# A hybrid RWKV-7 / neighbourhood-attention step: the first modulation moves from VectorE to TensorE

## The reference, cut to what matters

```python
def modulation(cond, w_ada, b_ada):            # w_ada: 1024 x 6144
    m = jax.nn.silu(cond) @ w_ada + b_ada
    return jnp.split(m[..., None, :], 6, axis=-1)

sh1, sc1, g1, sh2, sc2, g2 = modulation(cond, lp['w_ada'], lp['b_ada'])
h = rmsnorm(x, lp['norm1_g']) * (1 + sc1) + sh1
z = h @ lp['w_in']                             # then RWKV-7, attention, w_out, ConvFFN
```

## Time and profile before

| what | value |
|---|---|
| time, median of 3 runs | 2557.2 us (2552.21 to 2563.93) |
| the profiled execution | 2560.71 us, its span 2558.7 us |
| TensorE busy | 2397.7 us, 94% of the span |
| VectorE, ScalarE, GpSimd busy | 52%, 28%, 26% |
| granted TensorE clock, mean | 0.981 |

### The profile page before, as it was taken

How to read it: one execution, slowest core, us unless ns; L and a number is a source line. 1 busy time by engine, 2 the same in 40 slices (tenths; PEclk the granted TensorE clock), 3 DMA queues, 4 the chain that set the end, 5 groups by cost and what they waited for, 6 DMA issues and landing times.

```text
span 2558.7 us, 50522 instructions
## 1 busy us (share of the span) xinstructions
PE 2397.7 (94%) x21498; PEld 1966.3 (77%) x21498; DVE 1331.7 (52%) x2126; ACT 720.0 (28%) x1179; POOL 654.0 (26%) x283
## 2 busy tenths in 40 slices
PE   1799999999999998889999998999999999999997
PEld 1677778788888887788855687788888888888886
DVE  7755656536467667896543323634333433443344
ACT  3272736444355554333300001201100110011002
POOL 0220210111111111222100243344343434444341
PEclk9899999999999999999989998999999999999998
DMA  6312131112257777676513310011111111011112
GB/s 250 103 53 73 45 108 54 35 74 77 97 171 195 207 202 207 179 209 177 175 66 113 118 42 25 25 42 35 41 41 34 42 34 42 33 42 34 41 34 91
DMA packets 225583, 234.50 MB, mean 92 GB/s; under 512 B 143922, under 2 KB 178866, under 8 KB 224946
## 3 DMA queue, kind: packets, MB, share of 16 engines
q1 hardware_dynamic: 200114, 229.54, 28.4%
q10 hardware_dynamic: 25344, 3.15, 0.8%
HBM read 173.79 MB, written 57.02 MB: 90 GB/s over the span
## 4 chain that ended last, share of the span: by engine, by line
PE 84%; DVE 8%; issue 3%; ACT 2%; DMA 1%; ACTq 1%; POOL 1%; SPq 0%; DVEq 0%; POOLq 0%
PE PS L860 21%; PE PS L862 20%; PE PS L861 20%; PE PS L1301 5%; PE PS L969 3%; PE PS L941 2%; PE PS L955 1%; DVE buffer L1997 1%; DVE buffer L1996 1%; PE PS L943 1%; PE PS L1021 1%; DVE buffer L1796 1%; ACTq L1671 1%; PE PS L1111 1%; PE PS L872 1%
## 5 line engine op out<-in xcount | busy, mean ns | idle before, releaser
L860 PE MATMUL PS<-buffer,buffer 128*128 128x512 f32 (+1 forms) x2784 | 1007.0, 362 | 21.0 <-POOL buffer L2269 8.3
L862 PE MATMUL PS<-buffer,buffer 128*128 128x512 f32 (+1 forms) x2784 | 998.1, 359 | 0.0
L861 PE MATMUL PS<-buffer,buffer 128*128 128x512 f32 (+1 forms) x2784 | 998.0, 358 | 0.0
L860 PEld LDWEIGHTS PS<-buffer,buffer 128*128 128x128 f32 x2784 | 527.0, 189 | 114.7 <-issue 19.3
L862 PEld LDWEIGHTS PS<-buffer,buffer 128*128 128x128 f32 x2784 | 526.9, 189 | 83.6
L861 PEld LDWEIGHTS PS<-buffer,buffer 128*128 128x128 f32 x2784 | 527.1, 189 | 82.6 <-issue 1.0
L2278 POOL TENSOR_TENSOR buffer<-buffer,buffer 128x1024 fp32r<-128x1024 f32 x76 | 184.3, 2424 | 836.2 <-PE PS L862 528.6
L2225 DVE SCALAR_TENSOR_TENSOR buffer<-PS,buffer,buffer 128x512 f32<-128x512 f32 (+1 forms) x264 | 158.5, 656 | 156.0 <-PE PS L862 156.0
L2279 POOL TENSOR_TENSOR buffer<-buffer,buffer 128x1024 fp32r<-128x1024 f32 x76 | 193.4, 2545 | 6.0
L2201 DVE TENSOR_SCALAR buffer<-buffer,buffer 128x1281 f32<-128x1281 f32 x22 | 34.4, 1566 | 292.7 <-ACT buffer L1752 292.7
L1752 ACT ACTIVATE buffer<-PS 128x512 f32<-128x512 f32 (+1 forms) x66 | 30.0, 529 | 514.7 <-PE PS L862 514.7
(11 more groups left out here) (217 smaller groups left out, 2802.3 us busy)
## 6 DMA issues: line engine op xcount, KB each, us to landing
buffer<-in_w_up SPq DMA_DIRECT2D x44, 512.0 KB, 3.3
buffer<-in_w_in SPq DMA_DIRECT2D x42, 512.0 KB, 5.0
ops_kept<-buffer SPq DMA_DIRECT2D x40, 512.0 KB, 5.1
buffer<-ops_kept SPq DMA_DIRECT2D x80, 256.0 KB, 3.5
buffer<-in_w_ada SPq DMA_DIRECT2D x32, 512.0 KB, 7.2
buffer<-rkv_kept SPq DMA_DIRECT2D x120, 128.0 KB, 3.4
buffer<-in_w_down SPq DMA_DIRECT2D x22, 512.0 KB, 3.3
buffer<-in_x SPq DMA_DIRECT2D x20, 512.0 KB, 9.8
```

What stands on the lines that cost most here:

```text
L860: mm(out, w_hi, x_hi, start=start, stop=False)
L861: mm(out, w_hi, x_lo, start=False, stop=False)
L862: return mm(out, w_lo, x_hi, start=False, stop=stop)
```

## The change: what it does

**The first modulation.** `w_ada`'s first 2048 columns are handed over in another order, `w_ada_first`: eight chunks of 1 MB, each with all 1024 input features (on partitions, in 8 blocks) for 256 output columns; chunk c holds columns of the shift for even c and of the scale for odd c, so that chunks 2m and 2m+1 serve the feature blocks 2m and 2m+1 of `h`. The conditioning vectors come as 16 more columns of the parameters. TensorE multiplies: for each chunk 8 float32 matmuls with the SiLU vector padded to 32 columns as weights and 256 columns of `w_ada` as the moving operand, the blocks k and k+4 into PSUM partitions 32*(k mod 4) and on (`modulation_parts`). VectorE copies the four partial rows out of PSUM (`parts_copied`), and TensorE adds and turns them with a 0/1 matrix of 2 columns (`modulation_sums`, two float32 matmuls). VectorE adds the bias (`modulation`) and makes the scales of a pair (`first_scale`).

**Order.** `x` is loaded before the chunks. TensorE makes the partial products of chunks 0 and 1 and their sums, and then for each pair m the partial products of the next pair's chunks, the transposes of block 2m, the sums, and the transposes of block 2m+1. ScalarE evicts the first and the middle segment, VectorE the last.

**Moved.** The broadcast load of the conditioning vectors and their SiLU (still needed for the other 32 blocks) now come behind the first stage: the load is issued after the last chunk's, the sigmoid comes after ScalarE's last rounding, the product after VectorE's last subtraction, and SyncE waits for it before it enters the loop. The first Q, K and V tiles are loaded ahead of that wait, and GpSimd splits them as soon as the last chunk's sums are made (`ada_made` 16); the query buffer is cleared after that.

**Places.** `FREE` is rounded up to a multiple of 16 words (64 bytes).

```diff
-        FREE = keep.at
+        FREE = -(-keep.at // 16) * 16
...
             for b in range(TB):
                 sp.dma_start(x10[:, b, :], dram["x"][b]).then_inc(tiles_moved[b // 2], 16)
+            def load_first(c):
+                if c >= 4:
+                    sp.wait_ge(ada_made, parts_made(c - 4))
+                sp.dma_start(ada_first[c % 4].rearrange("p k n -> p (k n)"), dram["w_ada_first"][c]).then_inc(ada_in[c % 4], 16)
+            for c in range(8):
+                load_first(c)
+            sp.wait_ge(sumsq_done, TB)
+            sp.dma_start(cond_raw.rearrange("p c k -> p (c k)"), dram["cond"].to_broadcast([P, 2 * D])).then_inc(cond_in, 16)
...
+            load_qkv(0)
+            sp.wait_ge(h_done, 3 * KB)
+            sp.wait_ge(cond_ready, 2)
...
+            def modulation_parts(c):
+                pe.wait_ge(ada_in[c % 4], 16 * (c // 4 + 1))
+                if c >= 2:
+                    pe.wait_ge(ada_used, sums_made(c - 2))
+                for k in range(KB):
+                    at = 32 * (k % 4)
+                    ins = mm(PS[at:at + 32, 6 + c % 2, 0:2 * P], cond_pad[:, k, :], ada_first[c % 4][:, k, :], start=k < 4, stop=k >= 4)
+                ins.then_inc(ada_made, 1)
+            def modulation_sums(c):
+                pe.wait_ge(ada_used, parts_made(c))
+                for b in range(2):
+                    ins = mm(PS[:, 6 + c % 2, 2 * P + 2 * b:2 * P + 2 * b + 2], ada_parts[c % 2][:, b * P:(b + 1) * P], sum_parts,
+                             start=True, stop=True)
+                ins.then_inc(ada_made, 1)
...
+            for m in range(KB // 2):
+                more = (2 * m + 2, 2 * m + 3) if m + 1 < KB // 2 else ()
+                for c in more:
+                    modulation_parts(c)
+                transposed(2 * m)
+                for c in more:
+                    modulation_sums(c)
+                transposed(2 * m + 1)
...
-            for n in range(ADA_FIRST):
-                if n == 11:
-                    dve.wait_ge(sumsq_done, TB + 1)
-                    V.link(dve.reciprocal(tokstat[:, 1, :], tokstat[:, 1, :]))
-                    for b in range(TB):
-                        ts(diag[:, b, :], ident, tokstat[:, 1, b:b + 1], None, ALU.mult).then_inc(diag_ready, 1)
-                V.link(ada_product(mod[:, n, :], 0, half, ada_spare))
-                ada_product(mod[:, n, :], 1, half, ada_spare).then_inc(ada_used, 1)
...
+            for m in range(KB // 2):
+                more = (2 * m + 2, 2 * m + 3) if m + 1 < KB // 2 else ()
+                for c in more:
+                    parts_copied(c)
+                last_segment(2 * m)
+                if m >= 1:
+                    rest_of_h(2 * m - 1)
+                for c in more:
+                    modulation(c)
+                if more:
+                    first_scale(m + 1)
+                last_segment(2 * m + 1)
+                rest_of_h(2 * m)
             rest_of_h(KB - 1)
+            dve.wait_ge(act_steps, 2)
+            tt(silu, silu, cond_raw, ALU.mult).then_inc(cond_ready, 1)
...
+            pool.wait_ge(consts_in, 32)
+            pool.wait_ge(ada_made, 16)
+            split_qkv(0)
+            pool.wait_ge(h_done, 3 * KB)
+            G.link(pool.memset(qbd[:, :, :], 0.0))
+            with G.loop(1, NP, 3) as i:
+                split_qkv(i)
```

More of the change, by code:

```diff
@@ L255, in build @@
         assert s2.at <= WORDS - 4 * D
-        ada_first = view(LO_AT, 4, 2 * D)
-        cond_raw = view(LO_AT + 8 * D, 2, D)
+        e1 = Space(UPPER)
+        ada_first += [e1(KB, 2 * P), e1(KB, 2 * P), view(WORDS - 4 * D, KB, 2 * P)]
+        e1 = Space(s2.at)
+        cond_sig = e1(KB, 2)
+        cond_pad = e1(KB, P // 4)
+        ada_parts = [e1(2 * P) for _ in range(2)]
+        assert e1.at <= WORDS - 4 * D
         ada_ring = [view(WORDS - 4 * D, D), view(WORDS - 3 * D, D), view(SCR_AT, D), view(SCR_AT + D, D)]
@@ L600, in attention @@
                 sp.dma_start(dram["new_v"][bass.ds(i, 1)].rearrange("a b s c -> s (a b) c"), vtok[:, 0:2, :]).then_inc(newkv_out, 16)
-            with sp.Fori(0, NP) as i:
+            with sp.Fori(0, NP - 1) as i:
                 attention(i)
+                sp.wait_ge(proj_done, (i + 1) * PROJ + 1)
+                load_qkv(i + 1)
+            attention(NP - 1)
             def load_tile(s, src, split=None):
@@ L862, in split_mm, with transposed @@
                 return mm(out, w_lo, x_hi, start=False, stop=stop)
-            pe.wait_ge(diag_ready, TB)
-            for k in range(KB):
+            def modulation_parts(c):
[12 more added lines that the diff above has]
+                ins.then_inc(ada_made, 1)
+            def transposed(k):
                 for g, (t0, n) in enumerate(SEGS):
@@ L1818, in scale_with_gain, with first_scale @@
                     .then_inc(ev, 1)
-            mod_blocks(0, ADA_FIRST)
-            dve.wait_ge(mod_done, 1)
-            scale_with_gain(gsc1, 8, "norm1", gsc_ready)
-            dve.wait_ge(gsc_ready, 1)
+            def first_scale(m):
+                dve.wait_ge(ada_used, sums_made(2 * m + 1))
+                part = gsc1[:, 2 * m:2 * m + 2, :]
+                V.link(ts(part, mod[:, KB + 2 * m:KB + 2 * m + 2, :], 1.0, None, ALU.add))
+                tt(part, part, par("norm1")[:, 2 * m:2 * m + 2].unsqueeze(2).to_broadcast([P, 2, 2]), ALU.mult).then_inc(gsc_ready, 1)
             def rest_of_h(k):
@@ L2260, in _, with split_qkv @@
             G = Steps(pool, pool_steps)
-            pool.wait_ge(h_done, 3 * KB)
-            pool.wait_ge(consts_in, 48)
-            G.link(pool.memset(qbd[:, :, :], 0.0))
-            with G.loop(0, NP, 3) as i:
+            def split_qkv(i):
                 for s in range(3):
@@ L2418 @@
         "w_ada": one["w_ada"].T.reshape(48, P, D),
+        "w_ada_first": one["w_ada"][:, 0:2 * D].reshape(KB, P, 2, 4, 2 * P).transpose(3, 2, 1, 0, 4).reshape(8, P, KB * 2 * P),
         "cond": np.concatenate([a["c_ctx"], a["c"][0]]).reshape(1, 2 * D),
```

142 lines of the change are left out of this document (83 added, 59 removed).

## The result

| what | before | after |
|---|---|---|
| median, us | 2556.1 (2552.2 to 2563.9, 4 runs) | 2516.6 (2510.9 to 2520.1, 4 runs) |
| profiled execution, its span | 2560.71, 2558.7 | 2510.91, 2509.1 |
| ratio | | 0.9839, 95% interval 0.981 to 0.9869 |

The change makes the kernel 39.5 us faster in medians.

What follows compares the result with a forecast made beforehand. TensorE, busy 94%, was taken as the bound, idle mainly before the bias product, where VectorE bounds 20 to 30 us. First stage 23 us, buffer places nothing: 2560.71 less 23 is 2537.7, in medians 2534; range 2500 to 2550.

Steps and rivals of the forecast that it cites:

- Loads, norms, diagonals: Start of the first stage: `x` loaded by 19.0 us, diagonals ready at 25.3 in place of 44.4.
- Partial products: TensorE's `w_ada` chunks in the first stage: 0.95 us each, twice that after TensorE idles; bounds 0.9 and 3.45.
- Column groups don't overlap: Rival on the first stage's chunks: 3.45 us each, so gain only 10 us, time 2547; chance 8%.
- Start of the splits: First stage: GpSimd begins its six splits of Q, K and V tiles at 47.8 us.
- The collision: Splits slow VectorE's five last low parts of `h`; TensorE starts projecting at about 65 us, bounds 58 and 69.
- No collision: Rival: GpSimd and VectorE interleave without loss; gain 31 us, time 2526 to 2527; chance 7%.
- SiLU and the `w_ada` loop: After the low parts: SiLU product done at 69, VectorE's products at about 97, TensorE waiting 1.5 us for them.
- First stage in all: Up to the bias product: it moves from 120.27 to about 97, 23 us gained, bounds 18 to 31.
- The places of the buffers: All split matmuls: moving inputs to a 64-byte multiple gains nothing; bounds 134 us gained to 26 us lost.
- Same place, steady stream: Rival: weights and inputs placed alike speed matmuls outside attention by up to 3.8 ns; 15 us, time 2519; chance 18%.
- The new places hurt: Rival: inputs and weights both on the multiple collide and slow each stream; 26 us lost, time 2560; chance 5%.
- 16 bytes off cost an extra beat per line: Rival on split matmuls: aligning the inputs gains the full 134 us, time 2400; chance 7%.

Runs made afterwards that it cites:

- inputs_16_far: The changed kernel with `FREE` 16 bytes past a multiple of 256, as in the kernel before; 2544.0 us in one run, against 2554.3 for the kernel before.
- before_64: The kernel before with `FREE` alone rounded up to 64 bytes, first stage unchanged; 2530.2 us against 2556.15, ratio 0.9892.
- after_16: The changed kernel with `FREE` 16 bytes past a multiple of 64; 2531.8 us, ratio 0.9912 to the kernel before.
- before_ring_16: The kernel before with `WORDS` raised so the ring's weight tiles stand 16 bytes past a multiple of 64; 2523.7 us against 2557.9, ratio 0.9865.
- after_24: The changed kernel with `FREE` left unrounded, 24 bytes past a multiple of 64; 2545.6 us, ratio 0.9956 to the kernel before.

## Why the prediction came out as it did

- **Loads, norms, diagonals.** Right: 25.1 against 25.3. The DMA engines ran at 425 GB/s here, a little over the 408 of the earlier trace rows.
- **Partial products.** Right: 1.07 and 1.93 against 0.95 and 1.9, from the one row with 64x64 quadrants; but idle time just before a chunk isn't what makes it slow, as the two chunks of 3.48 show. "Column groups don't overlap" is out.
- **Start of the splits.** Right: 47.88 against 47.8.
- **The collision.** Right in kind, short in size. Four of the five low parts came to 2.9 to 3.5, and "No collision" is out. But I counted only the five low parts. The two four-column scale operations have SBUF operands alone, they too waited 2.06 and 2.25, and they stand ahead of the last evictions; the first projection came at 69.5, past the 65 taken and half a microsecond past the bound of 69. The Trainium skill, "SBUF — State Buffer", section "SBUF: two separate sides", states that an operation of VectorE shares the port with GpSimd if it has two SBUF inputs or runs in a mode that uses two ports, and that the later one then waits for the whole instruction. The trace agrees: the PSUM evictions kept their 0.80, and each small operation ended with a split. I had reckoned with the two inputs alone; of the small operations one (L1881) has a single SBUF input beside its constants, and it waited like the other. Whether it ran in such a mode no row shows.
- **SiLU and the `w_ada` loop.** Right in kind: SiLU product done at 71.1 (69 forecast), bias product at 99.1 (97 forecast), the third load late. It was later than I had it: VectorE idles 2.45 for it. TensorE waited 0.2 us for VectorE, not 1.5, because it started its projections 4.5 later than forecast.
- **First stage in all.** 23 us forecast, at least 18. In the two spans 21.0. But kernels with the new first stage had the bias product at 99.1 to 102.8 in nine profiles, those with the old one at 118.0, 118.6 and 120.1; and inputs_16_far, the changed kernel with before's pitches, is 10 us below the kernel before on its chip (2544.0, one run, against 2554.3). The first stage is worth 10 to 21 us, 13.5 as the remainder of the medians (39.5 less the 26.0 of before_64), so my 23 was too much by several us, and even my lower bound of 18 was above that remainder. after's trace is among the quickest: its clock records start with full speed at 25.7 us and its third `w_ada` load landed at 83.05; in after_16 these were 31.1 and 86.49, and the bias product came at 102.5.
- **The places of the buffers: the step that failed.** "I take nothing", since 16 bytes hold four whole elements and float32 streams showed no loss. Measured: 26 us in medians. The bounds held it (nothing to 134), the value did not, and it is this term that put the forecast 17 us too high: 26 us not counted here, against some 9 too many in the first stage. That the error was not larger is luck, since the two partly cancel; the time lies in the wide range because that took in the rival of the steady stream. The Trainium skill ("SBUF — State Buffer", section "Specifications (TRN2)") gives lines of 16 bytes; what I read from it, that any multiple of 16 bytes is as good as another, did not hold: 229.3 against 234.6 ns with both places on multiples of 16 bytes.
- **The rivals.** "Same place, steady stream" was the mechanism, at 18%: weights and inputs lay differently in the ring's streams, and that cost 5.8 ns of 512 columns in the input projection and 4.2 in the rest (before against before_ring_16, where nothing else differs). The row that spoke for it was there, 231 against 235 in the earlier trace rows. I weighed it down with "attention also keeps its weights elsewhere" where its sum, 2519, was within 3 us of the result, though by chance: its first stage was some 10 too large and its stream some 11 too small. That the streams of attention also fell, 230.7 to 227.2, was in no case of mine. "The new places hurt" and "16 bytes off cost an extra beat per line" (2400) are both out: the best pitch seen, 226.9, is still 12 ns above 215.

## What to carry to other kernels

When two streams of one shape run at different pitches in one profile, that is a finding to be settled before anything else: look where the weights and the moving operand stand relative to each other, and try the same place within 64 bytes for both. Shift one of them by 16 bytes and measure, since alike was not the whole rule here; one number, `WORDS` or `FREE`, was worth 34 or 26 us, against 10 to 21 for all the rewritten first stage. And when work of GpSimd is drawn forward next to VectorE's, count every small SBUF operation between them as held for up to a whole GpSimd operation, and ask which wait ends last, on either engine, not which comes first.

## What the runs showed of the hardware

- An fp32r matmul of 512 columns took 227 to 235 ns in an unbroken stream on the full clock, by place alone, and 256 columns 113.5 (before_ring_16) to 120.5 (after_24). Moving the weights by 16 bytes (before_ring_16) made the kernel 1.35% faster.
- At 512 columns, weights and inputs alike within 64 bytes: 226.9 to 229.3 behind attention in all four placements tried; unlike: 231.1 to 234.6 in all six. At 256 columns the two kinds overlap: 113.5 to 119.6 alike, 116.7 to 120.5 unlike. Within attention, always alike: 227.2 to 227.3 at 0 and 32 bytes, 230.5 to 231.8 at 16, 233.4 at 24.
- VectorE's operations on 128x4 elements took 0.17 and 0.16 us alone, and 2.06 (one SBUF input) and 2.25 (two) beside GpSimd splits of 3.48 and 2.34 us. A low part took 2.91 beside a split and 1.48 beside GpSimd's clearing, which reads nothing.
- Sixteen instructions of 256 float32 columns on column groups of 128x32 took 1.07 us, 1.09 with neighbours in the same group, against 3.45 in a row: about four at a time.
- TensorE stood for 9.69 us up to 68.66. Its granted clock was 0.50 from 60 to 70 us and still 0.56 from 70 to 74 (1.2 GHz of 2.4), and its first matmuls of 256 columns came 0.21 us apart, against 0.118 later.
